# Dilated attention: the relative bias added in VectorE's pass for the maximum instead of by products on TensorE

## What is computed

```python
DIL_GROUPS = ((128, 1), (512, 4), (2048, 16))
def dilated_attention(q, k_blocks, v_blocks, q_gain, rel_bias, seq_len):
    q = rms_norm(q, q_gain)
    scale = 1.0 / math.sqrt(HEAD_DIM)
    outs, lses = [], []
    for g, (window, dil) in enumerate(DIL_GROUPS):
        ...
        mask, bias = band_mask_and_bias(window, dil, qb.shape[2], rel_bias[:, hs])
        logits = jnp.einsum('brnqhd,brnkhd->brnhqk', qb, kw).astype(jnp.float32) * scale
        logits = jnp.where(mask[:, None], logits + bias, NEG_INF)
        m = jnp.max(logits, axis=-1, keepdims=True)
        p = jnp.exp(logits - m)
        l = jnp.sum(p, axis=-1, keepdims=True)
        o = jnp.einsum('brnhqk,brnkhd->brnqhd', p, vw) / jnp.swapaxes(l, 3, 4)
        lse = jnp.swapaxes(m + jnp.log(l), 3, 4)
        ...
    weights = jax.nn.softmax(jnp.stack(lses), axis=0)
    return jnp.sum(weights * jnp.stack(outs), axis=0).astype(q.dtype)
```

## Time and profile before

| | us |
|---|---|
| median of 3 runs | 3321.79 |
| lowest and highest | 3318.90, 3325.92 |
| the profiled execution, its own time | 3322.76 |
| its span, first to last instruction | 3320.7 |
| busy in the span: TensorE products | 3271.2 |
| busy: VectorE | 1743.1 |
| busy: ScalarE | 1189.2 |
| busy: GpSimd | 414.3 |

### The profile page before, as it was taken

The page is one execution under the profiler, slowest core; times in us unless marked ns, Lnnn a source line. Parts: engine busy times, 40 slices in busy tenths (PEclk is TensorE's granted clock), DMA queues, the critical chain, the costliest instruction groups (busy, mean ns, idle before and its releaser), DMA issues.

```text
span 3320.7 us, 44519 instructions
## 1 busy us (share of the span) xinstructions
PE 3271.2 (99%) x18577; PEld 2617.0 (79%) x18577; DVE 1743.1 (52%) x2551; ACT 1189.2 (36%) x1884; POOL 414.3 (12%) x318
## 2 busy tenths in 40 slices
PE   8999999999999999999999999999999999999999
PEld 6777778887777888887777788888878887678887
DVE  7954456844446443448777544434464335454333
ACT  4344434534542422233233332223353224342221
POOL 0001012001001311113322111101011001011110
PEclk9999999999999999999999899999999999999999
DMA  6732123322122232342100023333323322023332
GB/s 243 232 95 69 53 95 120 114 84 64 58 89 70 90 100 95 96 130 83 52 2 2 27 87 112 97 95 95 96 89 95 95 91 85 7 73 98 99 96 83
DMA packets 83911, 295.47 MB, mean 89 GB/s; under 512 B 9472, under 2 KB 12800, under 8 KB 81664
## 3 DMA queue, kind: packets, MB, share of 16 engines
q1 hardware_dynamic: 78384, 270.61, 25.7%
q10 hardware_dynamic: 5328, 22.02, 2.1%
HBM read 283.94 MB, written 8.65 MB: 88 GB/s over the span
## 4 chain that ended last, share of the span: by engine, by line
PE 90%; DVE 5%; ACT 2%; issue 1%; POOL 0%; DMA 0%; ACTq 0%; DVEq 0%; POOLq 0%
PE acc L485 71%; PE acc L1529 1%; PE aux L1514 1%; PE acc L2515 1%; PE acc L3298 1%; PE aux L1810 1%; PE aux L3260 1%; PE aux L1828 1%; PE acc L1841 1%; PE acc L2519 1%; DVE w_lo L396 1%; PE acc L2502 1%; PE acc L2012 1%; PE aux L2001 1%; PE acc L2468 1%
## 5 line engine op out<-in xcount | busy, mean ns | idle before, releaser
L485 PE MATMUL acc<-op_hi,w_hi 128*128 128x512 f32 x2624 | 1070.0, 408 | 7.2 <-DVE op_lo L1166 3.8
L389 ACT ACTIVATE w_hi<-raw 128x1024 fp32r<-128x1024 f32 (+2 forms) x476 | 494.2, 1038 | 1522.0 <-PE acc L485 1512.1
L485 PE MATMUL acc<-op_hi,w_lo 128*128 128x512 f32 x2624 | 1025.7, 391 | 0.0
L485 PE MATMUL acc<-op_lo,w_hi 128*128 128x512 f32 x2624 | 1024.2, 390 | 0.0
L396 DVE TENSOR_TENSOR w_lo<-raw,w_hi 128x1024 fp32r<-128x1024 f32 (+2 forms) x476 | 574.3, 1206 | 288.5 <-ACT w_hi L389 288.2
L485 PEld LDWEIGHTS acc<-op_hi,w_hi 128*128 128x128 f32 x2624 | 493.9, 188 | 130.9 <-issue 30.1
L485 PEld LDWEIGHTS acc<-op_lo,w_hi 128*128 128x128 f32 x2624 | 494.8, 189 | 106.8 <-issue 10.1
L485 PEld LDWEIGHTS acc<-op_hi,w_lo 128*128 128x128 f32 x2624 | 493.6, 188 | 106.5
L485 PE MATMUL acc<-ffn_hi,w_hi 128*128 128x512 f32 x800 | 311.4, 389 | 0.0
L485 PE MATMUL acc<-ffn_hi,w_lo 128*128 128x512 f32 x800 | 311.2, 389 | 0.0
L485 PE MATMUL acc<-ffn_lo,w_hi 128*128 128x512 f32 x800 | 311.2, 389 | 0.0
(11 more groups left out here) (596 smaller groups left out, 3893.1 us busy)
## 6 DMA issues: line engine op xcount, KB each, us to landing
raw<-in_w SPq DMA_DIRECT2D x436, 512.0 KB, 3.6
late_ada<-in_ada ACTq DMA_DIRECT2D x32, 512.0 KB, 4.4
raw<-in_w SPq DMA_DIRECT2D x32, 384.0 KB, 3.0
ada<-in_ada ACTq DMA_DIRECT2D x4, 1024.0 KB, 14.7
ada<-in_ada SPq DMA_DIRECT2D x4, 1024.0 KB, 21.8
x_mid<-x SPq DMA_DIRECT2D x16, 256.0 KB, 2.9
x<-x_mid SPq DMA_DIRECT2D x2, 2048.0 KB, 7.9
skew<-rel_rows SPq DMA_DIRECT2D x12, 192.0 KB, 3.1
```

Source lines behind the costliest of these rows:

```text
L389: act.activation(self.w_hi[g % AHEAD][:, 0:k, :], self.raw[s][:, 0:k, :], ACT.Copy).then_inc(self.split_hi.handle, 1)
L485: mm = pe.matmul(self.bank(s, g), w[:, k, :], a[:, k, 0:s.n], start=(k == 0 and q == 0), stop=(k == k_tiles - 1 and q == 2))
```

## The change

The bias products go. The scores product of a unit with a bias is now complete by itself. VectorE takes, for each head, one `tensor_tensor_reduce`: it adds the bias table in SBUF to the scores in PSUM, multiplies by -1, writes this negated sum into `late_probs` in SBUF, and keeps the minimum over the keys, which is the negated maximum. ScalarE's exponential reads `late_probs` in place of the PSUM bank, with a scale of -1, and writes it in place. TensorE waits for that VectorE pass before it uses a bank again, and VectorE waits for the transposes of unit u - 2 before it writes into `late_probs`. Units without a bias are as before.

```diff
@@ scores(), TensorE
                 if u >= ring:
-                    pe.wait_ge(*self.exped.ge(2 * (u - ring + 1)))
-                n, bias = unit["keys"], unit.get("bias")
+                    pe.wait_ge(*(self.maxed if "bias" in unit else self.exped).ge(2 * (u - ring + 1)))
+                n = unit["keys"]
                 for e in range(2):
                     lhsT, rhs = unit["scores"][e]
-                    mm = pe.matmul(self.scores_bank(u, e)[:, 0:n], lhsT, rhs, start=True, stop=not bias,
-                                   skip_group_check=True)
-                    if not bias:
-                        mm.then_inc(*self.scored.inc())
-                for e in range(2) if bias else ():
-                    pe.matmul(self.scores_bank(u, e)[:, 0:n], core.c("ident"), bias[e], start=False, stop=True,
-                              skip_group_check=True).then_inc(*self.scored.inc())
+                    pe.matmul(self.scores_bank(u, e)[:, 0:n], lhsT, rhs, start=True, stop=True, skip_group_check=True
+                              ).then_inc(*self.scored.inc())
@@ exps(), ScalarE
-                    act.activation(self.probs[:, u % 2, e * n:(e + 1) * n], self.scores_bank(u, e)[:, 0:n], ACT.Exp,
-                                   bias=self.stat(u, 0, e), accum_out=self.stat(u, 1, e)).then_inc(*self.exped.inc())
+                    probs = self.probs[:, u % 2, e * n:(e + 1) * n]
+                    scores, sign = (probs, -1.0) if "bias" in unit else (self.scores_bank(u, e)[:, 0:n], 1.0)
+                    act.activation(probs, scores, ACT.Exp, scale=sign, bias=self.stat(u, 0, e),
+                                   accum_out=self.stat(u, 1, e)).then_inc(*self.exped.inc())
@@ maxima(), VectorE
                     dve.wait_ge(*self.scored.ge(2 * u + e + 1))
+                    if "bias" in unit:
+                        if u >= 2 and e == 0:
+                            dve.wait_ge(*self.turned.ge(u - 1))
+                        n = unit["keys"]
+                        dve.tensor_tensor_reduce(self.probs[:, u % 2, e * n:(e + 1) * n], self.scores_bank(u, e)[:, 0:n],
+                                                 unit["bias"][e], -1.0, FAR, ALU.add, ALU.min, self.stat(u, 0, e)
+                                                 ).then_inc(*self.maxed.inc())
+                        continue
```

More of the change, by code:

```diff
@@ L64 @@
 ROUND = 1.5 * 2.0 ** 23
+FAR = 3.0e38
 DECAY_SCALE = -float(np.exp(-0.5))
```

## The result

The change made the kernel slower. Over 18 runs of each the median went from 3321.58 to 3330.41 us, a ratio of 1.0029 with a 95% interval of 1.0017 to 1.0041. The forecast was 3311.8.

The account below looks back on a forecast made before the run. The prediction took TensorE's own order, busy 99% of the span, as the bound. Its terms, 3.2 + 5.9 + 2.3 - 0.5 - 0.6 = 10.3, called 10 us, took 3321.79 to 3311.8 us; range 3305 to 3322.

Parts of the forecast that it names:

- the sum by place: Gains and losses added over groups of units in the dilated attention stage: 10.3 us won, called 10 us.
- units 3, 4 and 16: Units where TensorE runs at 1.2 GHz; removed products priced at the upper clock, 2.3 us won.
- the fall of the clock through both long stretches: Rival: TensorE's lower level holds through stretches of 21.69 and 20.98 us, adding some 32 us, giving 3344 us; chance 0.08.
- turning points: For the falling clock: added time at the lower level of 20 us means no gain, 33 us slower by 0.2%.
- stays without a pause in its loop: Argument against the falling clock: between the gaps TensorE works without pause, and the clock came back at 2868 in such work.
- (b): VectorE's maximum becomes an adding, writing, reducing pass plus a fetch: 0.29 + 0.16 = 0.45 us for 128 columns.
- The lower end, 0.33: Lowest price of VectorE's pass with fetch, in us: about 0.25 for the maximum and 0.08 for the fetch.
- The dear pass as a rival: VectorE's pass costs near or above the scan: 4 us or less won; chance 0.24, shared with a further clock fall.
- the loss of 0.5 us at unit 1: At the stage's start, unit 1's two passes take 1.16 us where the maxima stand 0.66 before the copy.
- The step of the loop: One short unit in the loop: 2.02 us before, then 1.43 us set by VectorE, with TensorE at 1.38.
- Ten units: Units 10 to 12 and 17 to 23, without filling products: 0.59 us won each, 5.9 us together.
- the two VectorE-bound places: Units 0 to 2 and units 12 to 15: 0.5 and 0.6 us lost; about 1 us better at the lower price.

Follow-up runs that it names:

- e4: The changed kernel with filling products only in the gap at the start of the stage, against the kernel before: median 3323.1 us, ratio 1.0003.
- e2: The kernel before with its bias products left out, so bias and mask are missing from the logits, against the kernel before: median 3328.8 us, ratio 1.0021.
- e1: The changed kernel with all bias products still issued and overwritten by the scores, against the kernel before: median 3318.9 us, ratio 0.9997.
- e7: The changed kernel with both overwritten bias products in units 0 to 3, one in all others, against the kernel before: median 3323.4 us, ratio 1.0007.
- e8: The changed kernel run again beside the kernel before, with the clock of each run: median 3335.0 us, ratio 1.0042.
- e3: The changed kernel with two filling products in all 24 units instead of the first nine, against the kernel before: median 3336.5 us, ratio 1.0043.
- e6: The changed kernel with the start gap filled and one to three filling products in later units, against the kernel before: median 3327.9 us, ratio 1.0025.
- e10: The kernel before with filling products in the gap at the start, against the kernel before: median 3320.1 us, ratio 1.0003.
- e5: The changed kernel with overwritten bias products in units 0 to 3 and 10 to 23 only, against the kernel before: median 3321.4 us, ratio 1.0010.

## Why the prediction was wrong

**The step that failed** is the one on the granted clock in the sum by place: units 3, 4 and 16 were priced as if the low stretch kept its length (lower clock for 10 to 17 us in all), and the fall of the clock through both long stretches stood beside the forecast as a rival with a chance of 0.08. The profile shows 78 us at the lower level in the stage, and the runs 59 more each than before. That rival is what happened; it named the gaps and the removed products, and both counted. It overstated the price per us, one half where the runs show 0.35, and so gave 3344 for 3330. Its turning points are too early for the same reason: it put no gain at 20 us of added low time and slower by 0.2% at 33, and e4, with 37 us added, can't be told from the kernel before.

I held against it that TensorE "stays without a pause in its loop", and took the pauses for the cause. They are only a part of it. e4 fills the largest pause, which takes the low time from 107 to 85, and the level still falls; in e2 it falls in a loop whose pauses are 0.30 us. e1, e7 and the change form a row: with all, half and none of the products the low time is 50, 64 and 107 us. The row is not clean, since e7 keeps all products in units 0 to 3 and so the shorter gap at the start; against e4, with no products but the gap filled, it reads 50, 64 and 85. The rule of the Trainium skill that I cited (TensorE: Matmul & The Clock Gate, Part 1), that activity releases a throttle which is the default, agrees with this row. It can't be read off the busy time: from 2850 to 2860 the changed kernel's TensorE was busy throughout at 0.50.

**The price of the pass** (b) was 0.45 us and measured 0.22 between starts. I had added a fetch that in fact lies beside the next pass, and taken a whole duration for a distance. The lower end, 0.33, was still too high. The Trainium skill's figure (Vector Engine (DVE) Microarchitecture Reference, 5.2 Measured stream behaviour on trn2), from which I had worked out an estimate of 0.21 for the pass and 0.28 with a fetch, was the nearest: the 0.22 is its pass alone. The dear pass as a rival is thereby out. So is the loss of 0.5 us at unit 1: its two passes start 0.68 us ahead of the copy, where the maxima had started 0.66.

```profile
2847.51 0.40 DVE L3337 CUSTOM_DVE_ANT_0 late_probs<-aux,rel_bias 128x256 f32<-128x256 f32 x1
```

**The step of the loop** was 1.60 us at the upper level, not 1.43, but for another reason than VectorE's load: the wait of the values for the single output bank. The prediction did not look at it, because the bias products hid it. Ten units at 0.42 in place of 0.59 are 1.7 us less, and in the two VectorE-bound places the cheaper pass gives about 1 us back by the prediction's own lower price. So the 10.3 us at an unchanged clock were nearly right, as far as the estimate from e8 goes: 8.8, between 6 and 14.

**Right** were: ScalarE's longer read and the new waits cost nothing that e1 can measure; the mixing of units 12 to 15 stays VectorE's; the gap at the start gets longer.

**Open** is what in the bias products raises the mean, and why filling products of 512 columns come out worse over the runs (e3 and e6 against e1). The two kinds differ in their format (float32r and float32), in their length and in where they stand, and the fillings of e3 leave the gap at the start as it is; I did not part these. e3 together with e4's filling of that gap was not run, nor another output bank for the values.

## What to carry to other kernels

Before taking work from TensorE in a stage of small products, ask what its clock does in that stage: here some 16 us of products taken off TensorE gave about 9 us and cost about 21 in clock, by the estimate of e8. When the granted clock of a stage changes between two kernels, compare the time at the lower level over many runs, not one profile. To find out whether it is the product that is missed or its place that the new work took, issue it again with its result thrown away, as in e1.

## What the runs showed that I had not expected

- TensorE can be busy for 2.00 of 2.00 us in five windows on end (2850 to 2860) and stand at 1.2 GHz in all of them; in that profile it stood there for 61 us, busy for most of it.
- In e10's profile the level fell in the loop although TensorE was busy throughout and every bias product was there.
- Six units of 24 without their products, with fillings in them, added 12 us at the lower level (e5).
- The runs of one unchanged kernel spread over 24 us (3310.3 to 3334.5 in 35 runs), and the time of a run follows its low time with a correlation of 0.94 or more.
- A fused add, write and minimum over 128 columns takes 0.29 us, no longer than the plain maximum, and its fetch of 83 ns (the median) lies beside the next pass.
